# A decoder trunk whose split weights sit in two rings: each ring slot padded by 128 bytes

## The reference

```
xn  = rmsnorm(h, g_mix[i])
mix = attn_mixer(xn, ...) if i % 2 == 0 else rglru_mixer(xn, ...)   # projections in and out
h   = h + mix
h   = h + (silu(xn2 @ wg) * (xn2 @ wu)) @ wd          # xn2 = rmsnorm(h, g_ffn[i])
h   = h + sigmoid(rmsnorm(h, g_ple[i]) @ w_ple_gate[i]) * (p[i] @ w_ple_proj[i])
```

## Time and profile before

| what | value |
|---|---|
| two timed runs | 2493.55 and 2494.09 us, median 2493.82 us |
| span of the profiled execution, first to last instruction | 2493.2 us |
| PE busy | 2466.9 us (99%), 11084 matmuls |
| PEld busy | 1991.3 us (80%) |
| DVE busy | 1315.8 us (53%) |
| ACT busy | 1139.8 us (46%) |
| memory read and written | 440.49 MB and 2.10 MB, 178 GB/s over the span |

### The profile page before, as it was taken

How to read it: one execution, slowest core, us unless ns; L and a number is a source line. 1 busy time by engine, 2 the same in 40 slices (tenths; PEclk the granted TensorE clock), 3 DMA queues, 4 the chain that set the end, 5 groups by cost and what they waited for, 6 DMA issues and landing times.

```text
span 2493.2 us, 29756 instructions
## 1 busy us (share of the span) xinstructions
PE 2466.9 (99%) x11084; PEld 1991.3 (80%) x11084; DVE 1315.8 (53%) x1677; ACT 1139.8 (46%) x1533; POOL 3.2 (0%) x17
## 2 busy tenths in 40 slices
PE   8999999999999999999999999999999999999997
PEld 7888778888888888888887887888888888888886
DVE  5545665544444454444556676554454454444455
ACT  5425554544444444444454575444444444344454
POOL 0000000000000000000000000000000000000000
PEclk9999999999999999999999999999999999999999
DMA  7744435666666665555557445566666666555563
GB/s 225 219 115 121 133 119 183 180 186 184 184 185 180 185 184 185 185 185 185 179 186 237 134 156 175 183 185 180 184 185 184 185 180 185 185 186 185 185 202 134
DMA packets 234042, 443.87 MB, mean 178 GB/s; under 512 B 16184, under 2 KB 21344, under 8 KB 233824
## 3 DMA queue, kind: packets, MB, share of 16 engines
q1 hardware_dynamic: 233904, 442.62, 58.1%
q10 hardware_dynamic: 48, 0.02, 0.0%
HBM read 440.49 MB, written 2.10 MB: 178 GB/s over the span
## 4 chain that ended last, share of the span: by engine, by line
PE 98%; DMA 1%; DVE 1%; ACT 0%; issue 0%; ACTq 0%; DVEq 0%
PE ps L1275 30%; PE ps L1276 30%; PE ps L1277 30%; PE ps L1231 2%; PE ps L1486 1%; PE ps L1399 1%; PE ps L1330 1%; DMA raw<-in_w_in_rec_dram 1%; PE ps L1411 0%; PE ps L1436 0%; PE ps L1437 0%; PE ps L1438 0%; DMA h<-in_x_dram 0%; PE ps L1370 0%; PE ps L1360 0%; DVE w_lo L773 0%
## 5 line engine op out<-in xcount | busy, mean ns | idle before, releaser
L773 DVE TENSOR_TENSOR w_lo<-raw,w_hi 128x1024 fp32r<-128x1024 f32 x820 | 998.6, 1220 | 1092.3 <-ACT w_hi L536 1091.5
L536 ACT ACTIVATE w_hi<-raw 128x1024 fp32r<-128x1024 f32 x820 | 863.0, 1055 | 1159.5 <-PE ps L1277 1137.0
L1275 PE MATMUL ps<-w_hi,xa_hi 128*128 128x512 f32 x1664 | 659.3, 396 | 0.0
L1276 PE MATMUL ps<-w_lo,xa_hi 128*128 128x512 f32 x1664 | 656.9, 395 | 0.0
L1277 PE MATMUL ps<-w_hi,xa_lo 128*128 128x512 f32 x1664 | 656.9, 395 | 0.0
L1277 PEld LDWEIGHTS ps<-w_hi,xa_lo 128*128 128x128 f32 x1664 | 312.1, 188 | 76.2
L1276 PEld LDWEIGHTS ps<-w_lo,xa_hi 128*128 128x128 f32 x1664 | 312.2, 188 | 75.0
L1275 PEld LDWEIGHTS ps<-w_hi,xa_hi 128*128 128x128 f32 x1664 | 312.1, 188 | 75.0
L1275 PE MATMUL ps<-w_hi,xb_hi 128*128 128x512 f32 x864 | 352.8, 408 | 4.4 <-DVE xb_lo L836 2.3
L1276 PE MATMUL ps<-w_lo,xb_hi 128*128 128x512 f32 x864 | 342.1, 396 | 0.0
L1277 PE MATMUL ps<-w_hi,xb_lo 128*128 128x512 f32 x864 | 342.0, 396 | 0.0
(11 more groups left out here) (200 smaller groups left out, 1044.0 us busy)
## 6 DMA issues: line engine op xcount, KB each, us to landing
raw<-in_w_ffn_gate_dram SPq DMA_DIRECT2D x176, 512.0 KB, 3.7
raw<-in_w_ffn_up_dram SPq DMA_DIRECT2D x176, 512.0 KB, 3.7
raw<-in_w_ffn_down_dram SPq DMA_DIRECT2D x176, 512.0 KB, 3.6
raw<-in_w_in_attn_dram SPq DMA_DIRECT2D x88, 512.0 KB, 3.7
raw<-in_w_ple_gate_dram SPq DMA_DIRECT2D x64, 512.0 KB, 3.7
raw<-in_w_in_rec_dram SPq DMA_DIRECT2D x64, 512.0 KB, 3.9
raw<-in_w_out_attn_dram SPq DMA_DIRECT2D x32, 512.0 KB, 3.8
raw<-in_w_out_rec_dram SPq DMA_DIRECT2D x32, 512.0 KB, 4.4
```

What stands on the lines that cost most here:

```text
L536: nc.scalar.activation(w_hi[:, s, 0:n], raw[:, s, 0:n], ACT.Copy).then_inc(hi_ready, 1)
L773: nc.vector.tensor_tensor(w_lo[:, s, 0:n], raw[:, s, 0:n], w_hi[:, s, 0:n].bitcast(F32), ALU.subtract).then_inc(lo_ready, 1)
L1275: nc.tensor.matmul(o, xh[:, k, tok], w_hi[:, s, wk], start=(k == 0), stop=False)
L1276: nc.tensor.matmul(o, xh[:, k, tok], w_lo[:, s, wk], start=False, stop=False)
```

## The change

The rows of the two split rings become 32 elements (128 bytes) longer than the 1024 that are used. A slot then begins 4224 bytes behind the one before it. `w_hi` still begins at 49280, so its four slots are at 128, 256, 384 and 0 modulo 512. `w_lo` begins at 66176, which is again 128 modulo 512, and its slots have the same four remainders. `raw` is not padded and does not move. Every tensor behind the rings moves by 1024 bytes and keeps its remainder modulo 512. The instructions, their order on each engine and their waits are the same as before, but for one line number more.

```
+WROW = 2 * CW + 32
...
         raw = put("raw", [NRING, 2 * CW])
-        w_hi = put("w_hi", [NRING, 2 * CW], F32R)
-        w_lo = put("w_lo", [NRING, 2 * CW], F32R)
+        w_hi = put("w_hi", [NRING, WROW], F32R)
+        w_lo = put("w_lo", [NRING, WROW], F32R)
```

## The result

The changed kernel takes 2473.06 us (median of 2472.89 and 2473.23) against 2493.82 before: 20.8 us less, ratio 0.9918 with a 95% interval of 0.9898 to 0.9938. The span of the profiled execution fell from 2493.2 to 2471.5 us.

What follows compares the result with a forecast made beforehand. PE's matmuls were taken to bound the kernel; PE's own work 0 and covered work 0 left the span at 2493.2 us, plus 0.6 us for the median: 2493.8 us, range 2486.5 to 2501, no change at 0.86.

Steps and rivals of the forecast that it cites:

- What bounds the kernel: PE, busy 2466.9 of 2493.2 us; the time is 9792 matmuls at 0.2333 us, 2285 us, plus 208 us of other pieces.
- ACT, DVE and the transfers at nothing: Ring accesses by ACT and DVE change by zero, at most some 0.04 us each and hidden; SP's transfers to `raw` change nothing.
- the 20 ns above 512 columns: Pitch 0.2333 us against 0.2133 for 512 columns; the excess stays while ACT and DVE are idle, so not from them.
- two readings of the earlier trace: The 6.7 ns step with `pT`: the stationary operand's own start (sum zero), or the reads' distance (16.2 us per place, either way).
- PE's moving read at nothing: The 512-column reads from the rings, a quarter still starting at 128 modulo 512 afterwards, were taken to change by zero.
- The one from steps of 512: Operand blocks step by 512, 1024 and 2048 bytes at an unchanged 0.23 us pitch, so only distances below 512 stay open.
- the plainer difference: Alignment to 128 bytes, `pT` at 128 and `xa` at 448 modulo 512, preferred over distance as the cause of the 6.7 ns.
- That a change under 2% can hardly be told from none: A change under 2%, about 50 us, was taken as about what a measurement can tell from none.
- a cheaper class in some places: Rival: distance counts, one to three ring places go from 0.2333 to 0.2267 us: 2477.6, 2461.4 or 2445.2 us; chance 0.05.
- the windows by place: Sign that distance counts: four consecutive slots become unequal, 2.72 us in a cheaper place, 2.88 dearer, 2.56 without the excess.
- the whole 20 ns goes: Rival: the excess depends on the moving read's start; two or three places lose it, 2397 or 2348 us; chance 0.04.
- The rule of the Trainium skill: Moving operand and weight load have independent SBUF read ports; by that the distance can't matter and the sum is zero.

Runs made afterwards that it cites:

- mixed kernels: Against the kernel before, ring slots padded by 32 or 16 bytes and starts moved, giving each place its own distance: 2480.42, 2491.51, 2482.99 and 2476.38 us.
- uniform ones: Against the kernel before, rings left alone and activations moved to 128 or 64 modulo 512, one distance in all places: 2434.17 or 2453.35 us.

## Why the prediction was wrong, point by point

*What bounds the kernel* was right: the gain is PE's (21.3 of the 21.7 us of the span), and the long waits keep their order.

*ACT, DVE and the transfers at nothing* was right: 1.06 and 1.23 us per split, and DVE's and ACT's busy totals within 0.4 us of those before.

*That the 20 ns above 512 columns do not come from the other engines* was right for the part that the runs moved. The kernel with the same start for both reads has ACT and DVE at the same work and a slot of 2.72 us, so 6.7 of the 20 ns are the distance. What the other 13.4 are is open.

*The step that failed* is the choice between two readings of the earlier trace rows. The prediction saw the cheaper pitch with `pT` and put it down to the stationary operand's own start (448 being no multiple of 128), which the change leaves alone, so it put PE's moving read at nothing. The runs showed the other reading, the distance between both reads, which took 4.4 ns off half of the matmuls: moving both together changes nothing (1.0001), moving the activations alone gives 0.9764 or 0.9837. Two arguments carried the wrong choice. The one from steps of 512 (distances by multiples of 512 don't matter) was true but said nothing on steps of 128. And the plainer difference was taken for the likelier cause, though the same rows fitted both; its chance should have been nearer to that of the forecast than 0.05.

*That a change under 2% can hardly be told from none* was wrong: the interval of the ratio is 0.2% to either side, and the gain of 0.8% is clear of it.

*The rival "a cheaper class in some places"* is what happened: two places of four, in the windows by place that the prediction named as its sign. Its price was too high. It put 6.7 ns on a place, the step to distance 0, but the two places came to distance 64, which is worth 233.3 − 228.9 = 4.4 ns: 4848 matmuls × 4.4 = 21 us, against 20.8 measured and 32.4 at the price that the prediction had. That the 21 fits so well is partly luck: by the starts in both traces, places 1 and 3 save 19.4 us and places 0 and 2, behind them, 2.3.

*The rival "the whole 20 ns goes"* fell for the distances tried: at the best of them 226.7 ns are left, 13.4 above the 213.3 that 512 columns take at 2.4 GHz by the earlier trace rows.

*The rule of the Trainium skill* that the prediction weighed, in "TensorE: Matmul & The Clock Gate", section "Step-by-step: what each phase is for", says that the weight load has a read port of its own and takes nothing from the running matmul. What the prediction drew from it, that the distance between the reads can't matter, is what the runs disprove for this type and shape: with the rings left alone and only the activations moved, the time goes from 2493.83 to 2434.17 us. Whether the load takes bandwidth from the moving read is not shown: halving one load in three gave nothing back.

## What to carry to other kernels

When PE is the bound and its starts are further apart than its columns explain, the distance between the moving and the stationary operand in SBUF, modulo 256 bytes, is worth a try; it costs a few bytes of padding. These runs show it for one kernel, with float32r operands and a stationary operand loaded anew for each matmul. Here the cheap remedy was to start both at the same remainder (192 bytes in front of the activations, 2434 us), not to spread the slots of a ring, which puts half of the matmuls on a good distance and half on a bad one. And when two rows differ in two things at once, as `pT` and `xa` did, neither thing is excluded by being the less plain one.

## What the runs showed of the hardware that was not expected

- With float32r operands, 512 moving and 128 stationary columns at 2.4 GHz, the pitch depends on the distance of the two operands' starts (moving minus stationary) modulo 256 bytes: 226.7 ns at 0, 228.9 at 64, 233.3 at 192. The order counts: 64 and 192 are equally far apart, in opposite directions. At half clock, at distance 192, there was nothing above 512 columns.
- The dependence is not smooth: 16, 32 and 96 are each dearer than 0 and 64 beside them (slots of 2.777, 2.803 and 2.811 us, measured in mixed kernels, against 2.720 and 2.747 in uniform ones). Why is open.
- Halving one stationary load in three left the pitch as it was at distance 192 (ratio 1.0001) and lengthened it at distance 0 (2461.71 us against 2434.17).
- A change of distance works on for a few matmuls: behind a slot at a good distance, the first matmuls of a slot at a bad one are still cheap. In places 0 and 2 of the changed kernel the first two steps are 230 and 226 ns in the median, the later ones 236 and 231 by turns. The other way, a slot at distance 0 behind dear ones takes 2.744 to 2.765 us instead of 2.720.
